# Leaving the filling products out of the mix loop's three waits (two-block transformer, one core)

## The reference

```python
for l in range(DEPTH):                       # DEPTH = 2
    h = rms_norm(x, g_mix_norm[l])
    z = h @ w_in[l]
    a = mla_mixer(q_lat, kv_lat, k_rope, ...)    # 4 heads, causal softmax over 512 keys
    gm = sgu_mixer(uv, g_sgu_v[l], ...)          # u * (w_spatial @ v)
    po = pool_mixer(pin, w_pool[l], ...)         # window means, 64x64 products
    mix = concat([rms_norm(a), rms_norm(gm), rms_norm(po)])
    x = x + mix @ w_out[l]
    h = rms_norm(x, g_ffn_norm[l])
    x = x + (silu(h @ w_gate[l]) * (h @ w_up[l])) @ w_down[l]
```

## Time and profile before

| | |
|---|---|
| time, median of 3 runs | 2576.8 us (2576.75, 2576.8, 2578.47) |
| profiled execution, its own time | 2578.25 us |
| its span, first to last instruction | 2576.4 us |
| PE busy | 2551.7 us, 99% of the span |
| POOL busy | 1836.8 us, 71% |
| DVE, ACT busy | 1063.0 us, 476.7 us |
| mean granted clock of TensorE | 0.998 |

### The profile page before, as it was taken

How to read it: one execution, slowest core, us unless ns; L and a number is a source line. 1 busy time by engine, 2 the same in 40 slices (tenths; PEclk the granted TensorE clock), 3 DMA queues, 4 the chain that set the end, 5 groups by cost and what they waited for, 6 DMA issues and landing times.

```text
span 2576.4 us, 31893 instructions
## 1 busy us (share of the span) xinstructions
PE 2551.7 (99%) x11848; PEld 2128.5 (83%) x11848; DVE 1063.0 (41%) x1657; ACT 476.7 (19%) x894; POOL 1836.8 (71%) x1846
## 2 busy tenths in 40 slices
PE   9999999999999999999999999999999999999998
PEld 8688888887788888888888888888988998888887
DVE  7643331047433220443530412795378254404325
ACT  5432110034421110201100102300300032100013
POOL 6757777667577776777776776687667777867763
PEclk9999999999999999999999999999999999999999
DMA  5112222231122222222322222222122203222221
GB/s 176 49 66 98 98 93 100 92 113 66 50 98 98 98 98 98 82 98 99 105 98 98 98 98 101 85 96 98 66 67 96 98 34 107 98 98 98 98 98 66
DMA packets 39439, 236.46 MB, mean 92 GB/s; under 512 B 4416, under 2 KB 8000, under 8 KB 12096
## 3 DMA queue, kind: packets, MB, share of 16 engines
q1 hardware_dynamic: 37488, 232.55, 26.1%
q10 hardware_dynamic: 1872, 2.80, 0.3%
HBM read 233.24 MB, written 2.10 MB: 91 GB/s over the span
## 4 chain that ended last, share of the span: by engine, by line
PE 96%; DVE 3%; ACT 0%; issue 0%; POOL 0%; DVEq 0%; ACTq 0%; POOLq 0%
PE psum L714 30%; PE psum L715 30%; PE psum L716 30%; PE psum L1252 1%; PE psum L1116 1%; PE psum L1202 1%; PE psum L1132 1%; PE psum L1208 0%; PE psum L1234 0%; PE psum L744 0%; DVE qk L2085 0%; DVE qk L2086 0%; PE psum L1149 0%; PE psum L1402 0%; PE psum L989 0%
## 5 line engine op out<-in xcount | busy, mean ns | idle before, releaser
L543 POOL TENSOR_TENSOR w_low<-w_stage,w_high 128x512 fp32r<-128x512 f32 x836 | 1123.5, 1376 | 17.4
L538 POOL TENSOR_SCALAR w_high<-w_stage 128x512 fp32r<-128x512 f32 x836 | 554.8, 691 | 597.5 <-PE psum L716 595.9
L714 PE MATMUL psum<-x_high,w_high 128*128 128x512 f32 (+1 forms) x1680 | 657.0, 391 | 0.0
L716 PE MATMUL psum<-x_high,w_low 128*128 128x512 f32 (+1 forms) x1680 | 650.4, 387 | 0.0
L715 PE MATMUL psum<-x_low,w_high 128*128 128x512 f32 (+1 forms) x1680 | 650.4, 387 | 0.0
L715 PEld LDWEIGHTS psum<-x_low,w_high 128*128 128x128 f32 x1680 | 315.5, 188 | 66.5 <-issue 2.6
L714 PEld LDWEIGHTS psum<-x_high,w_high 128*128 128x128 f32 x1680 | 315.5, 188 | 66.4 <-issue 2.6
L716 PEld LDWEIGHTS psum<-x_high,w_low 128*128 128x128 f32 x1680 | 315.5, 188 | 64.7
L1907 DVE TENSOR_TENSOR psum<-psum,x_res 128x512 f32<-128x512 f32 x64 | 44.8, 700 | 459.1 <-PE psum L716 455.9
L714 PE MATMUL psum<-mlp_high,w_high 128*128 (+1 forms) x576 | 224.1, 389 | 0.0
L715 PE MATMUL psum<-mlp_low,w_high 128*128 (+1 forms) x576 | 224.1, 389 | 0.0
(11 more groups left out here) (320 smaller groups left out, 3415.1 us busy)
## 6 DMA issues: line engine op xcount, KB each, us to landing
w_stage<-in_wstream SPq DMA_DIRECT2D x213, 1024.0 KB, 4.9
w_stage<-in_wstream SPq DMA_DIRECT2D x12, 256.0 KB, 5.4
x_res<-in_x SPq DMA_DIRECT2D x8, 256.0 KB, 5.6
out_x<-x_res SPq DMA_DIRECT2D x16, 128.0 KB, 1.8
ple_proj<-in_p ACTq DMA_DIRECT2D x2, 512.0 KB, 3.8
inv_count_sb<-in_inv_count SPq DMA_DIRECT2D x1, 512.0 KB, 4.5
inv_count_sb<-in_inv_count ACTq DMA_DIRECT2D x1, 512.0 KB, 4.2
qk<-in_mask ACTq DMA_DIRECT2D x1, 306.0 KB, 2.7
```

What stands on the lines that cost most here:

```text
L538: last = pool.tensor_scalar(wh[:, s, part], stage[:, s, part], 1.0, 1.0, ALU.mult, ALU.mult)
L543: last = pool.tensor_tensor(wl[:, s, part], stage[:, s, part], wh[:, s, part].bitcast(F32), ALU.subtract)
L714: pe.matmul(out, wa, ra, start=start, stop=False)
L716: return pe.matmul(out, wb, ra, start=False, stop=stop)
```

## The change

The calls that issue the filling products in this loop are gone: `spread_norm(p, 2, 6)` is now `spread_norm(p, 2)`, with its default of none, and the call of `busy_work` ahead of the wait for `probs_ready` is removed. The waits themselves, the semaphores and the products that are read stay as they are.

```diff
-                between = {5: pool_products, 7: gate_products, 11: lambda: token_sum(p, 2, 2), 13: lambda: spread_norm(p, 2, 6),
+                between = {5: pool_products, 7: gate_products, 11: lambda: token_sum(p, 2, 2), 13: lambda: spread_norm(p, 2),
                            14: lambda: token_sum(p, 3, 2)}
...
                         take(p, b)
-                        busy_work(b, {10: 5, 14: 7}.get(r, 0))
                         pe.wait_ge(probs_ready, L * steps + r + 1)
```

## The result

| | before | changed |
|---|---|---|
| median | 2577.26 us (9 runs) | 2584.75 us (9 runs) |
| lowest to highest | 2576.72 to 2578.47 | 2582.89 to 2586.96 |
| ratio, 95% interval | | 1.0028, 1.002 to 1.0036 |
| profiled execution, its span | 2578.25, 2576.4 us | 2584.6, 2582.8 us |
| mean granted clock | 0.998 | 0.993 |

The change made the kernel 7.5 us slower, 0.28%. One execution of the kernel before, timed beside the last two experiments, took 5227.52 us; it counts in no ratio, but it does in the median of 2578.17 given there (the other twenty have 2577.86).

What follows compares the result with a forecast made beforehand. PE was taken as the bound, busy 2551.7 of 2576.4 us. No direct gain, plus clock-fall losses of 2.0 + 1.2 = 3.2 us a layer, 6.4 in two, on 2576.8 gave 2583.2 us; range 2578.7 to 2588.5.

Steps and rivals of the forecast that it cites:

- Nothing direct is gained: At the waits of t = 12, 13 and 16, removing fillers gains 0 to 0.12 us in all, taken as 0.
- second place: Waits after t = 16's scores, ahead of 128.20 (r = 15): clock falls in about half the executions, 1.2 us a layer.
- first place: Waits of t = 12 and 13, ahead of `spread_norm` at 118.56: clock falls in nearly every execution, 2.0 us a layer.
- Price: Loss from slow work behind both places: 2.0 us plus 1.2 (2.35, in half the executions), 3.2 a layer, 6.4 in two.
- The base: Whole kernel before: median 2576.8 us taken as starting time, the profiled execution of 2578.25 lying 1.45 us above it.
- How long the clock stays low: After a fall at either place: open term, bounded by 3.4 and 6.8 us.
- Signs that failed as written: Transposes of r = 15 1-3 us past 128.20; same length 130 to 630; `spread_norm` within 0.1 us of POOL's copy.
- That the clock holds: Rival: neither place brings the clock down; time stays 2576.8 us, or 2576.7 with the direct gain; chance 0.10.
- the short-stretch case: Rival: only single short low stretches, or fewer places; 2.2 to 3.7 us lost, 2579.0 to 2580.5; chance 0.27.
- The self-feeding case: Rival: after 118.56, values and one-column sums keep the clock low, to 128.2 and beyond; about 2588 us; chance 0.15.
- The rule of the Trainium skill: Only idle gaps between matmul bursts longer than any left here (2.35 us at most) lower the clock; time stays 2576.8.

Runs made afterwards that it cites:

- the last two experiments: Against the kernel before (2578.17 us): layer 0's fillers removed, layer 1's kept, 2582.03 us; two 384-column products added per layer ahead of one-column sums (L989), 2577.78 us.
- the emptied second place: Kernel before with only the seven fillers of t = 16 removed, the eleven of t = 12 and 13 kept: 2580.95 us against 2578.14, ratio 1.0011.
- first place alone: Kernel before with the eleven fillers of t = 12 and 13 removed, the seven of t = 16 kept: 2581.79 us against 2578.14, ratio 1.0013.
- thin fillers: Kernel before with 6, 7 and 8 one-column products on `ones` replacing the 512-column fillers at the three waits: 2589.42 us against 2578.14, ratio 1.0048.

## Why the prediction was right

- **Nothing direct is gained.** Right. With the clock held, the emptied second place kept its times to 0.04 us and the emptied wait of t = 13 to 0.06 us, and emptying t = 13 alone did not make the kernel faster. The waits end when DVE and POOL say so. One reading was loose: the seven fillers of t = 16 end by their record at 126.92, 0.28 us after DVE's division (126.64) and not within 0.1; the run with this place emptied shows that nothing hung on it.
- **The clock falls at the first place in nearly every execution, at the second in about half.** The first half is right: in the profiles with the first place empty (changed kernel, first place alone, layer 0 alone) it fell there in five of five cases. The second was put too low: in the profiles it fell there in three of five cases (twice in the changed kernel, once with layer 0 emptied, not at all with the second place alone emptied), but that last execution was a fast one, and the median loss of 2.8 us speaks for a fall in nearly every layer. Nine executions of the changed kernel between 2582.89 and 2586.96 say that none went without falls.
- **Price: 2.0 us at the first place, 1.2 at the second, 3.2 a layer.** Measured in the profile 1.66 and 1.78, 1.44 and 1.49: 3.1 and 3.3 a layer, 6.4 in all, the very sum predicted. That is partly luck. At the first place I had the fall between 116 and 119; it came at 114.0, before the wait for POOL began, and the low clock was long, so that 2.7 of its 6.8 us were hidden and 4.1 lay over work. In other executions a long stretch came later and cost more (2.49 and 1.95 us in the run with the first place alone emptied), or it was short. At the second place two errors cancelled: I had a price of 2.35 and multiplied it by one half, where the falls of this profile cost 1.45 each and came in both layers.
- **The base.** I took the median of three, 2576.8. Of all nine it was 2577.26, and the changed kernel's median is 7.5 us above it where I said 6.4. The medians are worse than the one profile by 1.1 us. The profile before (2578.25) had a fall of its own at 41.9, and six of the nine executions lie 1 us or more below it, at 2576.72 to 2577.27; the profile after had one at 571, so in the profiles these two cancel.
- **How long the clock stays low** I had left open between 3.4 and 6.8 us. Both occur, at both places (compare the changed kernel and the run with layer 0 alone emptied), and with thin fillers it was at least 10.0.
- **Signs that failed as written.** The transposes of r = 15 start at 127.98 and not 1 to 3 us after 128.20, since the changed execution ran 1.92 us ahead when it reached the scores of t = 12; clear of that, they come 1.7 us later. Between 130 and 630 the traces are not of the same length, for the fall at 571 adds 1.5 us. `spread_norm` begins 0.15 us after the end of POOL's copy (116.57 to 116.72), not within 0.1.
- **The rivals.** That the clock holds is refuted by the four falls in the profile; the short-stretch case would be 2.2 to 3.7 us, below the interval of 5.2 to 9.3 us (0.002 and 0.0036 of 2577.26). The self-feeding case did not come in the changed kernel's profile: the clock was back at 120.9 and 131.1, through the values and one-column sums. A low stretch could reach into the values (until 133.3 with layer 0 alone emptied), but none went on past them.
- **The rule of the Trainium skill** that I weighed (page "TensorE: Matmul & The Clock Gate", section "Why this matters for your kernels") would have kept the time. Here the measurement decides against it: no gap of PE in the changed kernel's loop was longer than 2.19 us, and with thin fillers the clock fell at 115.4 though PE's longest gap since 107.7 was 0.85 us. The same page's section "A second HAM failure mode: psum-queue depth-cycling" reports of another kernel that frequent short idle times between groups of matmuls made the clock swing between its two levels. The four low stretches of the changed kernel, which began in gaps of 0.89 to 2.19 us, are in line with that.

## What to carry to other kernels

A product whose result nobody reads can be worth more than its time: look at the granted clock around PE's waits before you delete work that "only" fills one. Here fillers were free while they ended before the releaser did (compare the start of the next instruction with the end of what it waits for), and cost 0.23 us each beyond that. Products of 512 columns kept the clock up; products of one column did not, and stretched when it was down; no width between was tried. Fill every wait of a group or measure what a partly filled one does: once the clock is down, the fillers that are left take almost twice as long and can outlast their wait. Fill only as much as is needed: by the median, 14 products did here nearly what 36 do.

## What was not expected of the hardware

- The clock fell to 0.50 with PE and its weight loads recorded as busy for 6.60 and 5.94 of 6.60 us (thin fillers). The busy share of the records alone did not tell whether the clock would hold.
- The kernel before has a fall of its own at 41.9, and five of the other profiles have one near 570, where no edit reaches (568.9 to 572.8), of about 1.5 us each. They are probably a good part of the spread from 2576.3 to 2580.2 us on one chip, and a difference between two profiles must be cleared of them first. Not all of the spread is the clock's: in the ten profiles without a fall at 41.9 whose program is the same up to the scores of t = 12 in layer 0, these start anywhere from 111.83 to 113.03.
- In the emptied wait of 3.3 us, with PE at work for 0.95 of them, the clock could hold in both layers of one execution and fall in both of another.
